# An MoE kernel on one core: the tables of the further token blocks made behind the last expert, and nine unread products at the stage boundary where there were 24

## The chip, the cores and the metric

The kernel runs on one core of a Trainium2 chip. The metric is the device time of one execution in microseconds (us), as the median of three runs; beside it stands one execution that the hardware profiler recorded. Engines are named as the profile names them: PE (TensorE products), PEld (its weight loads), DVE (VectorE), ACT (ScalarE), POOL (GpSimd), SP (SyncE). A name with a q behind it (POOLq, PEldq) is that engine's sequencer, which handles branches, semaphores and drains by itself.

## The reference

One layer: a mixer (gated linear attention beside dilated attention) and, behind it, a mixture of experts with 32 experts, 4 of them for each of 512 tokens, width 1024. Only the second half and the last norm bear on the change. Cut to that:

```python
def moe(xn, router_w, router_b, w_gate_up, b_gate_up, w_down, b_down):
    logits = (xn @ router_w + router_b).astype(jnp.float32)
    top_v, top_e = lax.top_k(logits, TOP_K)              # 4 of 32 experts for each token
    gates = jax.nn.softmax(top_v, axis=-1)
    ...
    def expert_block(args):
        xb, e = args
        h = xb @ w_gate_up[e] + b_gate_up[e]
        gate = jnp.minimum(h[:, ::2], SWIGLU_LIMIT)
        up = jnp.clip(h[:, 1::2], -SWIGLU_LIMIT, SWIGLU_LIMIT)
        act = (up + 1.0) * (gate * jax.nn.sigmoid(SWIGLU_ALPHA * gate))
        return act @ w_down[e] + b_down[e]
    ...                                                  # each token: weighted sum over its 4 experts

h = h + moe(rmsnorm(h, norm_ffn_g), ...)
return rmsnorm(h, norm_final_g)
```

## The kernel before

The program is a row of stages. At the end of each, `stage` (L131) clears the semaphores of the stage and puts a barrier of all engines; the block of instructions that a stage consists of ends with a drain on each engine and a barrier of its own (L1277 for the stage that mixes and routes, L2047 for the experts' stage).

The stage `mix_and_route` ends with the router. DVE takes the top four of each token, counts each token's rank within its expert, and writes the addresses and records of a table of slots (L1668 to L1674). An expert has 96 first slots (`FIRST_SLOTS`). Should an expert have more tokens than that, the rest go through "further" blocks, which are run behind everything else, and only if there are any. Their tables are made by DVE: `further_places` (L1780) counts the blocks of each expert, writes their number to `n_further`, and gives each token beyond the 96 its place; `further_experts` (L2003) writes the expert of each further block. Before the change, the first is the last thing on DVE in `mix_and_route` (L1675), and the second stands on DVE behind the fourth chunk of expert 0 (L2164, L2165).

On PE the same stage ends with `no_work(24)` (L1458): 24 products of 512 columns whose result nobody reads. POOL ends it with the indirect gather of expert 0's rows (L1775).

The stage `experts` streams the weights of 32 experts as 12 chunks of 1 MB each through a ring of eight buffers. ACT rounds a chunk to its high half (`hi`, L1724), DVE subtracts to get the low half (`lo`, L1729), and PE multiplies rows-high by both halves and rows-low by the high half: `gate_up_chunk` (L1881, L1884) eight times for an expert, `down_chunk` (L1894, L1899) four times. In the meantime POOL scatters the table of slots with 16 small indirect transfers (L1759), reads it back, and then gathers each expert's rows (L1775) and adds each expert's output to the totals in memory (L1838). Experts 2 to 29 are in a loop of four to a turn. For the last expert the output isn't scattered: PE turns its one-hot matrix (L2240), DVE copies that out of PSUM (L2177), and PE adds the outputs with it (L2021, L2026). Then come the totals, the last norm (L2200, five instructions on DVE), and the stores.

Behind that, every engine runs `when_any` (L2300): it loads `n_further` from memory into a register (L2302), compares and branches (L2303) to the further blocks or past them. With these inputs no expert has over 96 tokens, so each engine takes the branch past them, and ends the stage with its drain (L2047).

## Time and profile before

| | us |
|---|---|
| median of 3 runs (lowest, highest) | 1821.55 (1821.44, 1821.83) |
| the profiled execution | 1821.84 |
| its span, first to last instruction | 1820.0 |
| PE busy in the span | 1790.7 (98%) |
| DVE, ACT, POOL busy | 1381.0, 1100.2, 141.1 |

The span is 1.8 us shorter than the execution's own time, and that execution is 0.29 us over the median. The mixer and the router take the span up to the boundary at 679 us; the experts' stage takes the rest. In the tables of the profile, busy is what an engine computes; waiting, branches and drains aren't counted, so that an engine can hold up a barrier without being busy.

### The profile page before, as it was taken

The numbers are of one execution on the slowest core, as the hardware profiler recorded it, in microseconds if no ns is written. First come the engines' busy times: TensorE is split into PE (matmuls) and PEld (weight loads), VectorE is DVE, ScalarE is ACT, GpSimd is POOL, SyncE is SP. The second block draws the span as 40 slices with busy tenths as digits, with TensorE's granted clock in tenths as the row PEclk, the third lists the DMA queues.
The fourth block names the chain that finished last, engine by engine and source line by source line (L and its number), as shares of the span: only waits on it lengthen the run. The fifth ranks groups of instructions, "written<-read, shape, count | busy, mean of one in ns | idle before, by whom it ended". The sixth has DMA issues, their size and how long they took to land.

```text
span 1820.0 us, 25032 instructions
## 1 busy us (share of the span) xinstructions
PE 1790.7 (98%) x9119; PEld 1472.9 (81%) x9120; DVE 1381.0 (76%) x1265; ACT 1100.2 (60%) x994; POOL 141.1 (8%) x120
## 2 busy tenths in 40 slices
PE   9999999999999999999999999999999999999996
PEld 7877788898888877788888888888888888888885
DVE  4256344337323568999999999999999999999997
ACT  4253222238331346777777777777777777777774
POOL 1000000000000017110000000000000000000001
PEclk9999999999999999999999999999999999999998
DMA  5321322211323558999999999999999999999993
GB/s 187 124 92 47 127 94 92 84 56 56 120 93 139 180 229 305 378 389 379 383 372 368 387 376 373 381 386 368 380 380 375 373 387 376 373 389 375 375 382 124
DMA packets 100601, 493.95 MB, mean 271 GB/s; under 512 B 15562, under 2 KB 17610, under 8 KB 51008
## 3 DMA queue, kind: packets, MB, share of 16 engines
q1 hardware_dynamic: 90640, 475.97, 68.3%
q0 software_dynamic: 9616, 16.62, 3.6%
q8 instruction: 37, 0.61, 0.1%
q10 hardware_dynamic: 288, 0.59, 0.1%
q14 instruction: 20, 0.16, 0.0%
HBM read 484.40 MB, written 25.21 MB: 280 GB/s over the span
## 4 chain that ended last, share of the span: by engine, by line
PE 58%; POOL 1%; DMA 1%; issue 1%; DVE 1%; ACT 0%; DVEq 0%; POOLq 0%
PE psum L1881 24%; PE psum L1894 12%; PE psum L1884 12%; PE psum L1899 6%; POOL slots_of_experts L1759 1%; PE psum L1853 1%; PE psum L1845 1%; PE psum L1874 1%; DMA h_sb<-normed_rows,row_index 1%; DMA slots_of_experts<-choice_token_and_weight,choice_row_of_table 0%; DMA lists_of_experts<-slots_of_experts 0%; DVE expert_chunk L2032 0%; DVE h_sb L2200 0%; DVE expert_lo L1729 0%; ACT expert_hi L1724 0%
## 5 line engine op out<-in xcount | busy, mean ns | idle before, releaser
L1729 DVE TENSOR_TENSOR expert_lo<-expert_chunk,expert_hi 128x2048 fp32r<-128x2048 f32 x384 | 865.7, 2284 | 45.2 <-ACT expert_hi L1724 42.6
L1724 ACT CAST expert_hi<-expert_chunk 128x2048 fp32r<-128x2048 f32 x384 | 734.9, 1916 | 225.8 <-PE psum L1884 187.6
L275 DVE TENSOR_TENSOR chunk_lo<-chunk,chunk_hi 128x2048 fp32r<-128x2048 f32 x48 | 109.9, 2290 | 252.9 <-ACT chunk_hi L271 252.7
L1881 PE MATMUL psum<-expert_hi,rowsT_hi 128*128 128x512 f32 x992 | 272.0, 396 | 0.0
L1884 PE MATMUL psum<-expert_lo,rowsT_hi 128*128 128x512 f32 x992 | 265.5, 389 | 0.5 <-DVE expert_lo L1729 0.5
L1881 PE MATMUL psum<-expert_hi,rowsT_lo 128*128 128x512 f32 x992 | 265.6, 389 | 0.0
L1884 PEld LDWEIGHTS psum<-expert_lo,rowsT_hi 128*128 128x128 f32 x992 | 186.1, 188 | 40.0 <-DVE expert_lo L1729 1.4
L1881 PEld LDWEIGHTS psum<-expert_hi,rowsT_lo 128*128 128x128 f32 x992 | 186.2, 188 | 39.6
L1881 PEld LDWEIGHTS psum<-expert_hi,rowsT_hi 128*128 128x128 f32 x992 | 181.5, 188 | 41.9 <-issue 7.6
L271 ACT CAST chunk_hi<-chunk 128x2048 fp32r<-128x2048 f32 x48 | 91.8, 1912 | 185.5 <-PE psum L306 158.1
L306 PE MATMUL psum<-chunk_hi,xT_hi 128*128 128x512 f32 x480 | 189.2, 394 | 4.3 <-ACT qk_rows_then_probsT L1070 1.7
L306 PE MATMUL psum<-chunk_hi,xT_lo 128*128 128x512 f32 x480 | 187.5, 391 | 0.0
L306 PE MATMUL psum<-chunk_lo,xT_hi 128*128 128x512 f32 x480 | 187.3, 390 | 0.0
L1894 PE MATMUL psum<-expert_hi,activationsT_hi 128*128 128x512 f32 x496 | 155.9, 396 | 0.0
L1894 PE MATMUL psum<-expert_hi,activationsT_lo 128*128 128x512 f32 x496 | 153.0, 390 | 0.0
L1899 PE MATMUL psum<-expert_lo,activationsT_hi 128*128 128x512 f32 x496 | 132.6, 389 | 0.0
L306 PEld LDWEIGHTS psum<-chunk_hi,xT_hi 128*128 128x128 f32 x480 | 98.0, 204 | 21.7 <-ACT qk_rows_then_probsT L1070 2.1
L306 PEld LDWEIGHTS psum<-chunk_hi,xT_lo 128*128 128x128 f32 x480 | 97.9, 204 | 16.4
L306 PEld LDWEIGHTS psum<-chunk_lo,xT_hi 128*128 128x128 f32 x480 | 98.0, 204 | 15.8
L1894 PEld LDWEIGHTS psum<-expert_hi,activationsT_lo 128*128 128x128 f32 x496 | 93.1, 188 | 20.0
L1899 PEld LDWEIGHTS psum<-expert_lo,activationsT_hi 128*128 128x128 f32 x496 | 93.1, 188 | 19.3
L1894 PEld LDWEIGHTS psum<-expert_hi,activationsT_hi 128*128 128x128 f32 x496 | 90.8, 188 | 17.2
(299 smaller groups left out, 1888.2 us busy)
## 6 DMA issues: line engine op xcount, KB each, us to landing
expert_chunk<-in_expert_w_gate_up SPq DMA_DIRECT2D x256, 1024.0 KB, 7.8
expert_chunk<-in_expert_w_down SPq DMA_DIRECT2D x128, 1024.0 KB, 6.9
chunk<-in_w_in SPq DMA_DIRECT2D x38, 1024.0 KB, 5.0
chunk<-in_w_branch_gla SPq DMA_DIRECT2D x4, 1024.0 KB, 5.0
chunk<-in_w_mix_out SPq DMA_DIRECT2D x4, 1024.0 KB, 5.1
gla_v<-in_x SPq DMA_DIRECT2D x4, 512.0 KB
y_glaT_away<-h_sb SPq DMA_DIRECT2D x1, 2048.0 KB, 7.7
att_qT_then_y_glaT<-y_glaT_away SPq DMA_DIRECT2D x1, 2048.0 KB, 7.6
```

Of the source, the lines that this page charges most:

```text
L271: act.copy(self.whi[c][:], self.raw[c][:]).then_inc(self.hi_done[c], 1)
L275: dve.tensor_tensor(self.wlo[c][:], self.raw[c][:], self.whi[c][:].bitcast(F32), ALU.subtract).then_inc(self.lo_done[c], 1)
L306: last = pe.matmul(bank, stationary, moving, start=(k == 0 and n == 0), stop=(k == KT - 1 and n == 2))
L1724: act.copy(self.expert_hi[c % self.SLOTS][:], self.expert_ring[c % self.RING][:]).then_inc(self.moe["hi"], 1)
L1729: dve.tensor_tensor(self.expert_lo[s][:], self.expert_ring[c % self.RING][:], self.expert_hi[s][:].bitcast(F32), ALU.subtract).then_inc(se ...
L1759: pool.indirect_dma_start(self.table, bass.IndirectOffsetOnAxis(ap=self.address[:, b, j:j + 1], axis=0), self.record[:, b, j, :], None, bo ...
L1845: last = pe.transpose(turned(f)[:, k, :], rows[taken, (HALF_KT * f + k) * P:(HALF_KT * f + k + 1) * P], self.ident[taken, taken])
L1853: last = pe.transpose(turned(f)[:, k, :], a[taken, (HALF_KT * f + k) * P:(HALF_KT * f + k + 1) * P], self.ident[taken, taken])
L1881: pe.matmul(bank, x[:, k, :], whi[s][:, m // 2, m % 2 * COLS:(m % 2 + 1) * COLS], start=False, stop=False)
L1884: last = pe.matmul(bank, rows_hi[:, k, :], wlo[s][:, m // 2, m % 2 * COLS:(m % 2 + 1) * COLS], start=False, stop=(k == KT - 1))
L1894: pe.matmul(bank, x[:, 2 * q + kk, :], whi[s][:, kk, m * COLS:(m + 1) * COLS], start=(q == 0 and kk == 0 and x is acts[0]), stop=False)
L1899: last = pe.matmul(bank, acts[0][:, 2 * q + kk, :], wlo[s][:, kk, m * COLS:(m + 1) * COLS], start=False, stop=(q == 3 and kk == 1))
```

## The change

- `further_places` goes from the end of `mix_and_route` to the end of the experts' stage on DVE, behind the four chunks of the last expert's down projection and ahead of the copy of the turned one-hot matrix. The wait for `tables_in` goes there too.
- `further_experts` goes from behind the fourth chunk of expert 0 to behind the last norm on DVE. Behind it DVE increments a new semaphore, `tables_made`.
- `when_any` now waits for `tables_made` on all five engines, ahead of the load of `n_further`.
- `no_work(24)` at the end of `mix_and_route` on PE becomes `no_work(9)`.

```diff
                 self.list_rows(pe, 0)
-                no_work(24)
+                no_work(9)
...
                 dve.tensor_tensor(self.record[:, :, :, 1], ex[:], tot[:].unsqueeze(2).to_broadcast([P, NB, TOP_K]),
                                   ALU.mult).then_inc(E_S["records"], 1)
-                self.further_places(dve)
...
                 lo(dve, 3)
-                dve.wait_ge(S["tables_in"], 32)
-                further_experts(dve)
                 for c in range(SLOTS, GU):
                     lo(dve, c)
...
                 for c in range(first, first + 4):
                     lo(dve, c)
+                self.further_places(dve)
+                dve.wait_ge(S["tables_in"], 32)
                 dve.wait_ge(S["hot_turned"], 1)
                 dve.tensor_copy(hotT[:], self.bank[6].rearrange("p (b n) -> p b n", n=P)).then_inc(S["hotT"], 1)
...
                         dve.scalar_tensor_tensor(out=fin[b][:, at], in0=self.total_sb[b][:, at], scalar=rs[:, b:b + 1],
                                                  in1=self.h[:, 3, at], op0=ALU.mult, op1=ALU.mult).then_inc(S["done"], 1)
+                further_experts(dve)
+                dve.sem_inc(S["tables_made"], 1)
                 further_dve(dve)
...
         def when_any(engine, body, first=None, then=None):
 
+            engine.wait_ge(self.moe["tables_made"], 1)
             n = engine.value_load(self.n_further[0:1, 0:1], min_val=0, max_val=self.FURTHER)
```

The next rows are the order of instructions on DVE in the built programs. The line numbers are those of each program (after the change they are one or two off), and the names behind "waits" are partly those under which an earlier stage used the same semaphore. First the end of routing and the start of the experts' stage, before the change:

```order
L1672 COPY choice_token_and_weight<-token_numbers_sb 128x16
L1673 TENSOR_TENSOR choice_token_and_weight<-top_exps,top_sums 128x16
L1784 TENSOR_SCALAR extra_blocks<-tokens_of_expert 128x32
L1786 TENSOR_SCALAR past<-tokens_of_expert 128x32 [waits chain_dve]
...
L1797 TENSOR_TENSOR place_in_further<-place_in_further,beyond_first_block 128x128 [waits chain_dve]
L1798 TENSOR_SCALAR place_in_further<-place_in_further 128x128 [waits chain_dve]
L1277 UNCONDITIONAL_BRANCH [waits chain_dve]
L2154 UNCONDITIONAL_BRANCH [waits barrier_Pool_Activation_PE_DVE_SP_release]
L1729 TENSOR_TENSOR expert_lo<-expert_chunk,expert_hi 128x2048 [waits gla_small_in]
```

and after it:

```order
L1672 COPY choice_token_and_weight<-token_numbers_sb 128x16
L1673 TENSOR_TENSOR choice_token_and_weight<-top_exps,top_sums 128x16
L1277 UNCONDITIONAL_BRANCH
L2153 UNCONDITIONAL_BRANCH [waits barrier_Pool_Activation_PE_DVE_SP_release]
L1728 TENSOR_TENSOR expert_lo<-expert_chunk,expert_hi 128x2048 [waits gla_small_in]
```

The 17 instructions of `further_places`, each of which waits for the one ahead of it, are gone from between the records and the branch that ends the stage. Now DVE behind the last expert's four chunks, before the change:

```order
L1729 TENSOR_TENSOR expert_lo<-expert_chunk,expert_hi 128x2048 [waits gla_small_in] x4
L2177 CAST slots_one_hotT<-psum 128x512 [waits gla_cleared]
```

and after it:

```order
L1728 TENSOR_TENSOR expert_lo<-expert_chunk,expert_hi 128x2048 [waits gla_small_in] x4
L1783 TENSOR_SCALAR extra_blocks<-tokens_of_expert 128x32
L1785 TENSOR_SCALAR past<-tokens_of_expert 128x32 [waits chain_dve]
...
L1796 TENSOR_TENSOR place_in_further<-place_in_further,beyond_first_block 128x128 [waits chain_dve]
L1797 TENSOR_SCALAR place_in_further<-place_in_further 128x128 [waits chain_dve]
L2176 CAST slots_one_hotT<-psum 128x512 [waits gla_cleared,x_turned,chain_dve]
```

The same 17 stand here now, ahead of the copy, which has two more semaphores to wait for. Last, the end of DVE's program, behind the last norm, as the change makes it; before it, the load of `further_blocks` stood right behind the L2200 rows and waited for nothing:

```order
L2199 SCALAR_TENSOR_TENSOR gate_values<-expert_chunk,total_rstd,h_sb 128x512
L2004 TENSOR_TENSOR blocks_before<-past,block_starts_sb 128x672
L2006 TENSOR_REDUCE block_expert_f<-blocks_before 128x21 [waits chain_dve]
L2007 TENSOR_SCALAR further_block_expert<-block_expert_f 128x21 [waits chain_dve]
L2304 TENSOR_LOAD further_blocks [waits chain_dve,moe_tables_made]
L2304 ISA x2
L2305 COMPARE_AND_BRANCH
```

On POOL the same load stands behind the four powers of the last norm:

```order
L2118 TENSOR_TENSOR total_rstd<-total_sum_squares,minus_half 128x1 [waits gla_y_out] x3
L2304 TENSOR_LOAD further_blocks [waits gate_up_lo,moe_tables_made]
L2304 ISA x2
L2305 COMPARE_AND_BRANCH
```

What moved is the wait: PE, ACT, POOL and SP go through the same load, two register instructions and branch as before, but each of them now behind DVE's `tables_made`.

## Rows read from the trace of the kernel before

**Rows 1.** The page, part 4: share of the chain that ended last, by engine

```profile
PE 58%; POOL 1%; DMA 1%; issue 1%; DVE 1%; ACT 0%; DVEq 0%; POOLq 0%
```

**Rows 2.** Waits of PE from 679 to 1800 us: total, times, longest

```profile
PE psum L1874 <- DVE rowsT_lo L1866: 1.0, 1, 1.0
```

**Rows 3.** Line 1277, sequencers: xcount: ns min/median/max, first to last start

```profile
L1277 POOLq DRAIN  x1: 4651/4651/4651, 672.1 to 672.1; - x1
L1277 PEldq DRAIN  x1: 5165/5165/5165, 673.4 to 673.4; - x1
L1277 DVEq DRAIN  x1: 10/10/10, 677.9 to 677.9; - x1
```

**Rows 4.** Timeline at the boundary, PE and POOL: start, us, engine, line [idle before]

```profile
670.71 7.87 PE L229 MATMUL psum<-ones_r 128*128 128x512 f32 x24
682.84 1.15 PE L1881 MATMUL psum<-expert_hi,activationsT_hi 128*128 128x512 f32 x4 [1.06 <-issue]
672.32 1.24 POOL L1775 DMA_INDIRECT h_sb<-normed_rows,row_index  x1 [5.43 <-issue]
```

**Rows 5.** Timeline at the boundary, DVE

```profile
673.60 0.16 DVE L1673 TENSOR_TENSOR choice_token_and_weight<-top_exps,top_sums 128x16 f32<-128x16 f32 x1
677.38 0.23 DVE L1798 TENSOR_SCALAR place_in_further<-place_in_further 128x128 f32<-128x128 f32 x1
679.51 2.29 DVE L1729 TENSOR_TENSOR expert_lo<-expert_chunk,expert_hi 128x2048 fp32r<-128x2048 f32 x1 [1.90 <-PEq L137]
681.72 1.01 DVE L1866 TENSOR_TENSOR activationsT_lo<-psum,activationsT_hi 128x384 fp32r<-128x384 f32 x2
```

**Rows 6.** Stretches: PE, PEld, DVE, ACT, POOL busy (instructions), clock, DMA, GB/s

```profile
668.50:675.30 6.80, 6.80 (x19) 5.17 (x18) 5.15 (x21) 5.27 (x6) 1.24 (x1) 0.50 0.07 16
675.40:678.60 3.20, 3.18 (x14) 2.26 (x13) 1.93 (x9) 0.00 (x0) 0.00 (x0) 1.00 0.09 37
```

**Rows 7.** Timeline of DVE in expert 0

```profile
691.43 0.85 DVE L2005 TENSOR_TENSOR blocks_before<-past,block_starts_sb 128x672 f32<-128x672 f32 x1
693.42 6.70 DVE L1729 TENSOR_TENSOR expert_lo<-expert_chunk,expert_hi 128x2048 fp32r<-128x2048 f32 x3
703.45 2.29 DVE L1729 TENSOR_TENSOR expert_lo<-expert_chunk,expert_hi 128x2048 fp32r<-128x2048 f32 x1 [1.17 <-ACT expert_hi L1724]
```

**Rows 8.** Timeline of POOL and DVE while the table of slots is written

```profile
703.85 2.75 POOL L1759 DMA_INDIRECT slots_of_experts<-choice_token_and_weight,choice_row_of_table  x1 [0.31 <-issue]
706.90 0.98 POOL L1759 DMA_INDIRECT slots_of_experts<-choice_token_and_weight,choice_row_of_table  x1 [0.30 <-issue]
```

**Rows 9.** Timeline of DVE behind the last expert

```profile
1787.63 8.89 DVE L1729 TENSOR_TENSOR expert_lo<-expert_chunk,expert_hi 128x2048 fp32r<-128x2048 f32 x4
1800.61 0.69 DVE L2177 CAST slots_one_hotT<-psum 128x512 fp32r<-128x512 f32 x1 [4.10 <-PE psum L2240]
1813.08 1.41 DVE L2200 SCALAR_TENSOR_TENSOR gate_values<-expert_chunk,total_rstd,h_sb 128x512 f32<-128x512 f32 x2
```

**Rows 10.** Lines 2302 and 2303, sequencers: the load of further_blocks, the branch

```profile
L2302 PEldq TENSOR_LOAD <-further_blocks x1: 486/486/486, 1802.9 to 1802.9; - x1
L2302 POOLq TENSOR_LOAD <-further_blocks x1: 499/499/499, 1811.7 to 1811.7; - x1
L2303 PEldq COMPARE_BRANCH  x1: 3654/3654/3654, 1803.8 to 1803.8; - x1
```

**Rows 11.** Line 2047, sequencers: the drains that end the experts' stage

```profile
L2047 PEldq DRAIN  x1: 73/73/73, 1807.5 to 1807.5; - x1
L2047 POOLq DRAIN  x1: 6513/6513/6513, 1812.6 to 1812.6; - x1
L2047 SPq DRAIN  x1: 7/7/7, 1817.3 to 1817.3; - x1
```

**Rows 12.** DMA issues from 679 to 1820 us: xcount, median us to landing

```profile
h_sb<-normed_rows,row_index POOLq DMA_INDIRECT x31
residual_rows<-h_sb,row_index POOLq DMA_INDIRECT x31, 10.0
```

More of the change, by code:

```diff
@@ L214, in build @@
                         "x_turned", "x_hi", "x_lo", "cleared", "passed", "weights_out", "hot_turned", "hotT", "y_hi",
-                        "y_lo", "totals", "padded", "table_cleared", "records", "placed", "lists_in", "half_set", "summed", "squared", "means", "powed", "done")}
+                        "y_lo", "totals", "padded", "table_cleared", "records", "placed", "lists_in", "half_set", "summed", "squared", "means", "powed", "done", "tables_made")}
                     self.residual_stored, self.normed_stored = self.sem("residual_stored"), self.sem("normed_stored")
```

## The prediction

> **What bounds the kernel now.** I read the page's chain first: PE takes 58% of it and no other engine over 1% [rows 1], so a microsecond counts where PE stands, or where nobody works because all wait for a barrier. The change touches two such places and a stretch between them. For the stretch I asked for PE's waits: in 1120 us of experts the longest but one is 1.0 us, at expert 2 [rows 2]. The rest is products one behind another, so the experts' stage is a block that slides with its start. The two places are its ends, and there the busy rows don't help, since drains aren't busy time; the sequencers' rows do.
>
> At the first boundary the barrier opens when the last engine has drained. A drain's row gives its start and its length, and the sum is when the engine was really done: PE 673.4 + 5.2 = 678.6, DVE 677.9, POOL 672.1 + 4.65 = 676.7 [rows 3]. PE is last, because of its 24 unread products, which run from 670.7 to 678.6 [rows 4]. DVE's last table instruction ends at 677.6, and its first work behind the barrier starts at 679.5 [rows 5]. So PE binds by 0.7 us over DVE and by 1.9 over POOL. POOL's row is the one to note: its last work is the gather of expert 0's rows, issued at 672.3 and generated by 673.6 [rows 4], and its drain still takes until 676.7.
>
> At the end of the kernel the same reading gives PE 1807.5 + 0.07 and SP 1817.3, but POOL 1812.6 + 6.5 = 1819.1 [rows 11], 0.9 us ahead of the span's end of 1820.0. So POOL's drain, which no table of busy time shows, ends the kernel. It starts that early because POOL loads the block count at 1811.7 [rows 10], right behind its last power, waiting for nobody.
>
> **The change, part by part.**
>
> The first boundary. `further_places` goes: DVE's records end at 673.8 instead of the tables at 677.6, 3.8 us earlier [rows 5]. PE's nine products: they start at 670.7 as before, and the clock is at 0.50 until 675.3 [rows 6]. At full clock a product takes 3.20 / 14 = 0.23 us; the other 10 of the 24 took the 4.6 us from 670.7 to 675.3, 0.46 each [rows 4, 6]. Nine take 4.1, so PE is done at about 674.9. POOL isn't touched: its gather waits for an index that DVE makes ahead of all this, so its drain ends at 676.7 as before. Now that one is last, and the barrier opens 678.6 - 676.7 = 1.9 us earlier, not the 3.7 us that PE and DVE leave room for. Bounds: 0 if POOL's drain has something in it that waits for the others, 3.7 if it goes with them. I take 1.9, since both of its rows are untouched. Behind the barrier the first low half and the turned rows' low half stand on DVE (679.5 to 682.7) [rows 5], and PE waits 1.06 us for them until 682.84 [rows 4]; this order stays, so all 1.9 us arrive at PE: **-1.9**.
>
> The clock. Before, PE ran products without a pause from 670.7, and the clock rose at 675.3 [rows 4, 6]; in the changed kernel the products end 0.4 us short of that, and then PE stands still until the barrier has opened, at about 677.6. If the clock isn't up by 680.9, when the first expert's products start, they run at half speed until it is. Lower bound 0, the clock rises as before. Upper bound: it needs the same 4.6 us of unbroken work again, counted from 680.9, and half of 4.6 is lost, 2.3 us; counted from the stage's start at 677.6 it is up at 682.2 and costs 0.65. There is little slack in which to make it good, the 1.0 us at expert 2 [rows 2], and even that hangs on a chain of POOL's which begins with PE's list for expert 1, behind the second chunk. In the likeliest case I put it at **+0.2**, near its lower end.
>
> `further_experts` leaves expert 0. It took 691.43 to 693.42, 2.0 us [rows 7]. Nothing comes of it: twelve microseconds later DVE stands for 1.17 us waiting for ACT, whose turn follows PE's [rows 7], so what DVE gains it waits away. There is a side effect to weigh. POOL writes the table of slots just then, and one such transfer takes 2.75 us where a low half runs on DVE (703.45 to 705.74) and 0.98 where none does [rows 7, 8]. The three table instructions left POOL alone; now the low halves come 2 us earlier and the gap behind them is 2 us longer. Sum of gaps the same, and both orders meet at the transfer under the low half of 703.45. **0**, bounds -0.5 to +0.5 (the wait of 1.0 us at expert 2 is all that could be won [rows 2]).
>
> `further_places` at its new place. DVE's four low halves end at 1787.63 + 8.89 = 1796.5, and the copy of the one-hot matrix waits 4.10 us for PE, until 1800.6 [rows 9]. The 17 instructions took 3.8 us behind one another [rows 5] and end at about 1800.4. They fit, with 0.2 us to spare for one more wait: **0**, at most +0.2. With that cover gone they'd cost up to 3.8.
>
> The end. Last on DVE is the norm's final piece, which ends at 1813.08 + 1.41 = 1814.5 [rows 9]. Behind it now `further_experts`, 2.0 us [rows 7], and the increment: `tables_made` is there at about 1816.5. What is queued behind the new wait on each engine is the load, the branch and the drain. POOL takes 0.95 us from load to drain (1811.7 to 1812.6) [rows 10, 11]: its drain starts at 1817.45. If it takes 6.5 us as before it ends at 1823.95, **+4.85**. PE is next: from the load at 1802.9 to the drain's end at 1807.6 are 4.65 us, 3.65 of them in the branch [rows 10, 11], hidden before behind the last norm. Now they end at 1821.15: without POOL the end would come +2.0 later. SP adds some 1.3 us of load and branch and is done before 1818. So POOL decides, and the question is whether those 6.5 us are work of the drain or a wait for something else. POOL issued 31 gathers, 31 scatters [rows 12] and 17 transfers for the table in this stage, 79 in all, and 6513 / 79 is 82 ns each; at the first boundary only one was out. A pass over what was issued would start when the drain starts, and would be as long as now. Bounds: 0 for the drain (the others' are 7 and 73 ns [rows 11]), and then PE's +2.0 is the end; 6.5 the other way. I take 6.5, its own row.
>
> Two rules of the Trainium skill bear on this. PE's branch took 3654 ns [rows 10], where POOL goes from its load through its branch to its drain in 0.95 us; "Runtime: NRT & Kernel Launch", section "Instruction fetch mechanics", says that a taken branch to a target outside the fetched window stalls until the page has been brought in. By that rule, the trace agrees, PE pays this again wherever its wait stands. POOL's drain took 6513 ns [rows 11]; "VectorE: DVE Perf Modes", section "The DRAIN you can't avoid", says that the drains of the frame around a program take about 12 ns each on all five engines. By that rule the drain's length is no work, the end would be PE's, and the kernel would come out level; the row of 6513 is against it as far as it goes.
>
> The sum is -1.9 + 0.2 + 0 + 0 + 4.85 = +3.15, so 1825.0 for the profiled execution of 1821.84. The median of the runs was 0.29 lower, and I predict for it: 1821.55 + 3.15 = 1824.7. A difference under 0.2%, 3.6 us, can't be told from none here.
>
> **Rivals.**
>
> First, the drain waits for something that the change doesn't move, and PE's branch is the end. This is the case that comes out not slower: -1.9 + 2.0 + 0 to 0.2, about 1821.8. For it: 6.5 us is long for an engine that has only four powers behind it, and 1819.1 is two microseconds behind the landing of the last store, which SP sees at 1817.3. Against it: the other long drain of POOL also went on for 3 us behind its last instruction, with no store near it [rows 3, 4], and nothing else of POOL's is out at the end. It decides if the drain's row in the changed kernel is shorter than 3.7 us. If PE's branch stall shrank too, it would be 1820.
>
> Second, the forecast with the clock low at the first expert, by the place and the price above: half rate from 680.9 for 1.3 to 4.6 us, +0.65 to +2.3 on top of +2.95, 1825.2 to 1826.8, about 1826.0. For it: nine products end before the clock rose in the trace of before, and the few ahead of them, from 668.5 on, had not raised it [rows 6]. Against it: 0.4 us is little, and one more turn of the unread products follows the barrier.
>
> Third, the change doesn't do what it says at the front: POOL's drain ends later for a reason that I don't see, and the barrier opens as before. Then only the end is left, 1821.55 + 4.85 = 1826.4.
>
> **How the numbers follow.** Forecast 0.42, 1824.7, its own range 1824.2 to 1825.3. First rival 0.25, 1820 to 1822.5. Second 0.27, 1825.2 to 1826.8. Third 0.06, 1826.4. The range takes in the forecast, the second and third, and the better part of the first: 1821.4 to 1826.8. Slower by over 0.2% is above 1825.2: most of the second rival, the third, and a little of the forecast, 0.34. Faster by over 0.2%, under 1817.9, none of the cases reaches: 0.03 for what I have overlooked. Within 0.2%: 0.63.
>
> **What would show it.** The first barrier: POOL's drain ends last, near 676.7, and DVE's first low half starts near 677.6 instead of 679.5. The end: five loads of `further_blocks` within 0.1 us of each other, about 2 us behind the last norm; PE's branch of about 3.6 us; POOL's drain of about 6.5 us, ending last. The forecast is wrong if that drain is short, or if the first products of expert 0 stand at twice 0.23 us each.

## The result, and the profile after

The changed kernel takes 1827.51 us (median of nine runs, 1826.39 to 1829.17), against 1821.58 for the kernel before on the same chip (nine runs, 1821.44 to 1822.01). The ratio is 1.0031, with a 95% interval of 1.0022 to 1.0040: it is slower by 5.9 us (4.0 to 7.3 by the interval). The forecast was 1824.7 and its range ended at 1826.8. The direction of the likeliest case was right, and the size was too small by 2.8 us. Two things stand beside each other here: the end, which came as forecast, and the middle, which did not.

The profiled execution of the changed kernel took 1828.05 us, with a span of 1826.3. Its line numbers are one or two lower than those of before (L1728 for L1729) or higher (L2304 for L2302).

**The front.** The sequencers' rows of the barrier's line in the changed kernel (count, ns, start), which answer to [rows 3]:

```profile
L1277 PEldq DRAIN  x1: 5180/5180/5180, 669.9 to 669.9; - x1
L1277 POOLq DRAIN  x1: 4581/4581/4581, 672.4 to 672.4; - x1
L1277 DVEq DRAIN  x1: 1267/1267/1267, 672.9 to 672.9; - x1
```

PE is done at 675.1, DVE at 674.1, and POOL at 672.4 + 4.6 = 677.0: POOL's drain is the last, as the prediction had it, and 0.3 us later than it had it. The DMA issues from 672.6 to 677.1 us tell what this drain waits for (the last number is the us from issue to landing):

```profile
h_sb<-normed_rows,row_index POOLq DMA_INDIRECT x1, 4.3
```

The gather of expert 0's rows is issued at 672.68 and has landed at 676.93, and the drain is over 81 ns later. In each of the twelve traces that hold this landing the drain ends 80 or 81 ns behind it. The timeline of PE behind it, with DVE's first low half (start, us, engine, line, then the idle time before it):

```profile
677.93 0.65 PE L1873 MATMUL psum<-bias_rows,ones_r 32*128 32x512 f32 x4 [2.85 <-PEq L137]
681.59 1.08 PE L1880 MATMUL psum<-expert_hi,activationsT_hi 128*128 128x512 f32 x4
```

```profile
677.93 2.29 DVE L1728 TENSOR_TENSOR expert_lo<-expert_chunk,expert_hi 128x2048 fp32r<-128x2048 f32 x1 [3.84 <-PEq L137]
```

The stage starts at 677.93 and not 679.51 [rows 5], 1.58 us earlier. But PE stood still for 2.85 us before it, where it was 0.93 us before. The windows tell what the clock did (the number ahead of the last two is the granted clock; these answer to [rows 6]):

```profile
668.00:674.70 6.70, 6.70 (x21) 5.47 (x20) 4.28 (x15) 5.74 (x6) 1.24 (x1) 0.50 0.08 21
674.80:678.10 3.30, 0.45 (x6) 0.20 (x4) 0.17 (x1) 0.00 (x0) 0.09 (x1) 1.00 0.19 65
678.20:681.50 3.30, 3.30 (x16) 2.66 (x13) 3.30 (x4) 0.96 (x2) 2.60 (x6) 0.50 0.48 181
746.50:749.70 3.20, 3.20 (x11) 2.24 (x8) 3.20 (x3) 1.12 (x2) 0.00 (x0) 0.50 0.98 394
```

The clock rose to its full 2.4 GHz at 674.7, nearly as the forecast had it. Then it stood at full while PE did nothing, and behind the pause it fell to 1.2 GHz for 3.4 us. That cost little here, since the fall ended at 681.6, where the first expert's products begin, and the slow products ahead of them filled time in which PE had waited for 1.06 us before the change: 681.59 for 682.84 [rows 4], so 1.25 of the 1.58 us arrive. The fourth row is another fall that the kernel before doesn't have, 65 us later, at expert 2.

**Expert 2.** PE's waits from 640 to 1800 us (total, times, longest), which answer to [rows 2]:

```profile
PE psum L1873 <- PEq L137: 2.9, 1, 2.9
PE psum L1873 <- DVE rowsT_lo L1865: 1.8, 1, 1.8
```

The one wait of 1.0 us that the prediction had called slack has become 1.8 us. DVE's row where it takes the lists of rows, first in the kernel before, then in the changed one:

```profile
729.25 0.15 DVE L1767 CAST row_index<-lists_of_experts 128x1 int32<-128x1 f32 x1 [2.18 <-DMA lists_of_experts<-slots_of_experts]
```

```profile
728.65 0.15 DVE L1766 CAST row_index<-lists_of_experts 128x1 int32<-128x1 f32 x1 [2.90 <-DMA lists_of_experts<-slots_of_experts]
```

DVE stands at this row until POOL's read of the lists has landed, with all its low halves queued behind. They came only 0.60 us earlier, and DVE waited 2.90 us for them instead of 2.18. PE in the changed kernel:

```profile
746.26 0.70 PE L1873 MATMUL psum<-bias_rows,ones_r 32*128 32x512 f32 x4 [1.80 <-DVE rowsT_lo L1865]
746.88 2.08 PE L1880 MATMUL psum<-expert_hi,rowsT_hi 128*128 128x512 f32 x4
750.18 1.07 PE L1883 MATMUL psum<-expert_lo,rowsT_hi 128*128 128x512 f32 x4
```

Before, the first of these stood at 746.84, so 0.58 us is left of the front's gain. The second row shows four products in 2.08 us where four at full clock take 1.07: the clock fell 0.15 us behind the pause of 1.80 us and came back 3.4 us later. By expert 3's first products the changed kernel is 0.94 us behind the kernel before (782.55 for 781.61), where it was 0.58 ahead at expert 2's: the fall cost 1.5.

**The end.** DVE's last norm and what is now behind it, then the loads and the drains (these answer to [rows 9], [rows 10] and [rows 11]):

```profile
1802.03 0.69 DVE L2176 CAST slots_one_hotT<-psum 128x512 fp32r<-128x512 f32 x1 [0.72 <-PE psum L2241]
1814.50 1.41 DVE L2199 SCALAR_TENSOR_TENSOR gate_values<-expert_chunk,total_rstd,h_sb 128x512 f32<-128x512 f32 x2
1815.83 0.85 DVE L2004 TENSOR_TENSOR blocks_before<-past,block_starts_sb 128x672 f32<-128x672 f32 x1
1817.60 0.18 DVE L2007 TENSOR_SCALAR further_block_expert<-block_expert_f 128x21 int32<-128x21 f32 x1
```

```profile
L2304 POOLq TENSOR_LOAD <-further_blocks x1: 497/497/497, 1817.9 to 1817.9; - x1
L2305 PEldq COMPARE_BRANCH  x1: 344/344/344, 1818.8 to 1818.8; - x1
```

```profile
L2046 POOLq DRAIN  x1: 6513/6513/6513, 1818.8 to 1818.8; - x1
L2046 PEldq DRAIN  x1: 72/72/72, 1819.2 to 1819.2; - x1
L2046 SPq DRAIN  x1: 13/13/13, 1819.4 to 1819.4; - x1
```

The norm ends at 1815.91, 1.43 us later than before. POOL's drain starts at 1818.84, 2.93 us behind the norm's end; before, it started 1.85 us ahead of it. That is 4.78, against the 4.85 of the prediction. The drain's length is the same to the nanosecond.

The ledger of the two profiled executions: expert 2's first products -0.58, the fall of the clock there +1.5, and +0.5 in the last expert (from its first products to the one-hot copy are 46.64 us for 46.19), together +1.43 at the norm's end; the end +4.78; sum +6.2, as the two executions differ (1828.05 for 1821.84).

### The profile page after: what moved, and what is told of

Its sections match the earlier page's. It is cut to its first block, busy times and chain, and to the rows that moved or that the text cites. A ratio compares the mean times of both kernels' runs of the same rounds, so it can differ in the third digit from the quotient of the medians.

```text
span 1826.3 us, 25002 instructions
## 1 busy us (share of the span) xinstructions
PE 1789.9 (98%) x9104; PEld 1472.2 (81%) x9105; DVE 1381.6 (76%) x1265; ACT 1100.8 (60%) x994; POOL 139.8 (8%) x120
## 4 chain that ended last, share of the span: by engine, by line
PE 58%; DVE 1%; POOL 1%; issue 1%; DMA 1%; ACT 0%; POOLq 0%; DVEq 0%
PE psum L1880 24%; PE psum L1893 12%; PE psum L1883 12%; PE psum L1898 6%; POOL slots_of_experts L1758 1%; PE psum L1852 1%; PE psum L1844 1%; PE psum L1873 1%; DVE expert_lo L1728 1%; DMA slots_of_experts<-choice_token_and_weight,choice_row_of_table 0%; DMA lists_of_experts<-slots_of_experts 0%; DVE expert_chunk L2031 0%; DVE h_sb L2199 0%; PE psum L2020 0%; POOL total_rstd L2118 0%
## 5 line engine op out<-in xcount | busy, mean ns | idle before, releaser
L1728 DVE TENSOR_TENSOR expert_lo<-expert_chunk,expert_hi 128x2048 fp32r<-128x2048 f32 x384 | 866.2, 2286 | 49.1 <-ACT expert_hi L1723 44.7
```

The source lines that it names most:

```text
L1728: dve.tensor_tensor(self.expert_lo[s][:], self.expert_ring[c % self.RING][:], self.expert_hi[s][:].bitcast(F32), ALU.subtract).then_inc(se ...
```

## The experiments

Fifteen runs followed, on four chips; e12 is the changed kernel again, and e15 repeats e9. On these chips the kernel before spread more than on the first one, from 1820.8 to 1825.2 us, with medians of 1822.3 to 1822.9, so each time is given beside the kernel before of its own chip, and the traces decide where a difference is under 2 us. Names: "later take" is the edit of e5. The intervals are for the ratio, 95%.

**e1, 24 products in the changed kernel.**

```diff
-                no_work(9)
+                no_work(24)
```

> The changed kernel with 24 unread products ahead of the barrier, not nine; the tables stay behind the last expert. Theory A, the clock: what the changed kernel lost beyond the end (about 2.9 us) comes of the pause that PE makes between its nine products and the first work behind the barrier. With 24 PE is the last to drain again (about 678.6), the clock rises once near 675 and stays, PE's wait at expert 2 is back to about 1.0 us: the front's gain goes and the loss in the middle goes too, 1821.6 + 4.8 = 1826.4, and the times lie within 0.6 us as before the change. Theory B, the order: the loss in the middle comes of further_experts having left expert 0 (the low halves there run earlier against POOL's transfers, so the lists come late). Then the wait at expert 2 stays near 1.8 us or more and the time is 1821.6 + 4.8 + about 1.5 to 3 = 1828 to 1829.4.

Measured: 1828.15 against 1822.88, ratio 1.0026 (1.0015 to 1.0037). The times don't separate the theories: 5.3 us above its own before, where theory A has 4.8 and the changed kernel 5.9, and the interval is 4 us wide. The trace does, and theory A is wrong as an account of the middle: PE pauses 0.93 us at the barrier and the clock stays up there, yet it waits 1.9 us at expert 2, and the clock falls at 748.3 for 3.4 us:

```profile
746.79 0.50 PE L1873 MATMUL psum<-bias_rows,ones_r 32*128 32x512 f32 x4 [1.89 <-DVE rowsT_lo L1865]
```

The absolute time lies in theory B's range only because the kernel before is 1.3 us slower on this chip; 5.3 is less than B's 6.4 to 7.8. B's reason is tested by POOL's rows: from the first of the 16 table transfers to the last are 34.84 us in this trace, and 34.84 in the kernel before. So `further_experts` in expert 0 neither helps nor hurts POOL.

**e2, nine products in the kernel before.**

```diff
-                no_work(24)
+                no_work(9)
```

> The kernel before with nine unread products, not 24; all tables stay where they were. DVE is then the last to drain, 677.9, 0.7 us ahead of PE's 678.6. Theory A (clock): PE stands still from about 675 to the barrier, the clock falls again behind it, and 0.7 us won are lost two or three times over: 1822 to 1824, with a wider spread. Theory B (order): nothing in the middle changes, -0.7, 1820.9.

Measured: 1823.24 against 1822.88 (median of ten; an eleventh execution took 9124.92 us and is left out), ratio 1.0003 (0.9994 to 1.0013). No difference by the times. The trace shows what the 0.6 us at the front turned into: PE paused 3.84 us, and the clock, which hadn't risen yet, stayed at half until 683.7.

```profile
678.92 0.80 PE L1874 MATMUL psum<-bias_rows,ones_r 32*128 32x512 f32 x4 [3.84 <-PEq L137]
682.75 1.53 PE L1881 MATMUL psum<-expert_hi,activationsT_hi 128*128 128x512 f32 x4
```

POOL's 16 transfers took 35.77 us, 0.9 longer, and the lists came at 730.4. Both the wait (1.87 us) and the fall at expert 2 are there, with the tables where they always were.

**e3, the tables where DVE was thought to have room.** `further_places` in expert 30 behind the fifth low half, `further_experts` and the increment ahead of the one-hot copy.

> The changed kernel with further_places in the middle of expert 30 and further_experts, with the increment of tables_made, in DVE's wait for the one-hot matrix: the tables are there at about 1800, so POOL's load waits for nobody. If the 4.8 us at the end are the delayed start of POOL's drain and nothing else, they go whole: 1827.5 - 4.8 = 1822.7, with POOL's drain of 6.5 us starting near its 1812.6. If the 17 + 3 instructions aren't hidden there, up to 3.8 us come back and the one-hot copy on DVE starts later than 1.4 us against the kernel before.

Measured: 1824.61 against 1822.88, ratio 1.0008 (0.9999 to 1.0017): 1.7 us above its own before, where the changed kernel stands 5.9. POOL's drain starts 1.84 us ahead of the norm's end again, so the end's 4.8 us go whole. The places aren't free, though. Of PE's waits the second is for an activation that DVE made late, behind the 17 table instructions; the first is for the rows of expert 2, whose gather took 11.7 us from issue to landing where it takes 8.3 in the changed kernel's trace, long before the tables' new places:

```profile
PE psum L1844 <- DMA h_sb<-normed_rows,row_index: 3.2, 1, 3.2
PE psum L1852 <- DVE h_sb L1976: 0.9, 1, 0.9
```

From expert 31's first products to the one-hot copy are 47.43 us here, 46.64 in the changed kernel and 46.19 in the kernel before.

**e4, the kernel before with a wait at the end alone.**

```diff
+                dve.sem_inc(S["tables_made"], 1)      # behind the last norm
                 further_dve(dve)
...
+            engine.wait_ge(self.moe["tables_made"], 1)
```

> The kernel before with the tables where they were, and the increment of tables_made behind the last norm, for which all five engines wait ahead of the load: it prices the wait at the end by itself. If POOL's drain is 6.5 us from wherever it starts: increment at 1814.5, drain from 1815.45 to 1821.95, 1821.6 + 2.85 = 1824.4. If it waited for something unmoved: 1821.6 to 1822. PE's branch takes 0.35 us (as in the changed kernel) and not 3.65, as the wait gives its fetch time.

Measured: 1823.65 against 1822.88, ratio 1.0005 (0.9996 to 1.0014): less than expected. The trace says why, and it is the expectation's mistake. DVE's increment doesn't wait for the norm's last write: the loads stand at 1813.3, while that write ends at 1815.37. POOL's drain starts 0.65 us ahead of the norm's end, 1.2 us later than before in that measure, and is 6513 ns long. PE's branch took 4.53 us here, so the wait ahead of it isn't enough to bring the 344 ns of the changed kernel; what they go with is said below.

**e5, the later take.** In expert 0, DVE takes expert 2's row numbers behind the low half of chunk 7 instead of ahead of it.

```diff
-                if q == 6 and more:
+                if q == (6 if e0 else 7) and more:
                     list_take(dve, e + 2, (e0 + 2) % self.UNROLL, reused=e0 > 1)
```

> The kernel before with one edit: in expert 0 DVE takes expert 2's row numbers one low half later (behind that of chunk 7, not ahead of it), so that the late lists don't hold up the low halves. Theory C, the lists: in every trace so far expert 2's first products start 17.6 us after DVE takes the lists, since DVE works without a pause in between; PE's wait there is the lateness of the lists. Then DVE gains its 2.2 us of idle time, PE's wait of 1.0 to 1.9 us goes, and the time falls by 1.0 or more, the slower executions the most. Theory A (the clock at the front alone): no change. If the gather of expert 2's rows is late in its turn, PE waits for it instead, 0.2 to 1 us at the transposes.

Measured: 1820.44 against 1822.45, ratio 0.9994 (0.9986 to 1.0003; one run of 1828.5 is in it). Nine of twelve runs lie between 1820.11 and 1820.88, but the interval takes in 1, so the trace has to show it. It has no wait of PE's at expert 2 at all, and DVE's 2.2 us have become 0.54:

```profile
729.78 0.15 DVE L1767 CAST row_index<-lists_of_experts 128x1 int32<-128x1 f32 x1 [0.54 <-DMA lists_of_experts<-slots_of_experts]
```

Theory C is shown: what PE waits for at expert 2 is the lists, through DVE's order.

**e6, the later take in the changed kernel.**

> The changed kernel with the same one edit. Theory C: PE's wait of 1.8 us at expert 2 goes and with it the 3.4 us at half clock behind it, worth 1.7: -3.5, 1827.5 to about 1824.0. Then what is left over the kernel before is the end's 4.8 less the front's 1.6 to 1.9, less the 1.0 that was won at expert 2. Theory A (the front's pause costs it): the loss stays, 1827 to 1828.

Measured: 1825.62 against 1822.45, ratio 1.0022 (1.0012 to 1.0031), 3.2 us above its own before where the changed kernel stands 5.9, so 2.7 went and not the 3.5 expected. The wait at expert 2 and the fall there are gone. The rest is at the front, where in this execution the fall lasted twice as long:

```profile
677.50:684.10 6.60, 6.22 (x22) 4.90 (x23) 6.16 (x6) 0.96 (x2) 5.34 (x7) 0.50 0.67 204
```

Against e5's trace this one starts the stage 1.55 us earlier and expert 31 0.02 us later (1752.99 for 1752.97), so the fallen clock cost 1.6 us. That is the second rival's mechanism, and a price inside its 0.65 to 2.3. The norm ends 0.49 us later than in e5, which is the price of `further_places`.

**e7, a longer pause on purpose.** Two more subtractions of 128x384 on DVE ahead of expert 2's low halves, in the kernel before.

> The kernel before with two more subtractions of 128x384 on DVE, into a tile that nobody reads, ahead of expert 2's low halves: 0.9 to 1.0 us more of PE's pause there, 1.9 instead of 1.0. If the pause makes the clock fall: +0.95 for the pause and +1.7 for 3.4 us at half rate, +2.6, 1824.2 on the chip of the first runs. If it doesn't: +0.95, 1822.6.

Measured: 1823.99 against 1822.45, ratio 1.0006 (0.9998 to 1.0015). Inconclusive: in the profiled execution the gather of expert 2's rows was late as well, so the pause came in two pieces of 1.39 and 1.22 us with 6.4 us of products between them, and the clock stayed up.

**e8, no powers on POOL.** The powers are replaced by copies on ACT, so this kernel leaves out the power that makes the last norm's scale.

> The kernel before without the four powers of the last norm; ACT copies the mean squares instead (so the output is not the reference's). POOL then has nothing behind the scatter of expert 30, and loads, branches and drains some 8 us earlier. If its drain is 6.5 us of work from wherever it starts, it ends by about 1811, SP's drain at 1817.3 is the last, and the kernel ends 1.8 us earlier. If the drain waits for the stores or for something else at the end, it gets longer, ends near 1819.1 as before, and nothing is won.

Measured: 1819.89 against 1822.45, ratio 0.9986 (0.9977 to 0.9995). The drains in its trace:

```profile
L2047 POOLq DRAIN  x1: 6513/6513/6513, 1799.5 to 1799.5; - x1
L2047 SPq DRAIN  x1: 13/13/13, 1817.2 to 1817.2; - x1
```

POOL drains 13 us earlier for the same 6513 ns, and SP's store is the end. The drain doesn't wait for the stores, which come behind its end. This trace also holds a pause of 1.81 us at expert 2 behind which the clock did not fall.

**e9 and e15, roots on ACT.** The kernel before with the later take, and with the last norm's four powers taken from POOL.

```diff
-                    pool.tensor_tensor(rs[:, b:b + 1], ss[:, b:b + 1], half[:], ALU.pow).then_inc(S["powed"], 1)
+                            act.activation(rs[:, m:m + 1], ss[:, m:m + 1], ACT.Sqrt).then_inc(S["powed"], 1)
...
+                    dve.reciprocal(rs[:, b:b + 1], rs[:, b:b + 1]).then_inc(S["inverted"], 1)
```

> The kernel before with expert 2's row numbers taken one low half later and, for the last norm, square roots on ACT and reciprocals on DVE in place of the four powers on POOL; all outputs are computed. POOL then loads, branches and drains behind the scatter of expert 30, near 1799. If the 6.5 us are work from wherever the drain starts, SP's drain is the last: 1.8 us less than with the later take alone (1820.4), about 1818.7. If the chain of root, reciprocal and two semaphores is longer than the power's, a few tenths come back. If the drain at the end waits for something else, nothing is won.

> The kernel before with the later take and the roots on ACT, again on this chip: 1818.8 (1817.8 to 1820.9 the first time), 1.8 us under the same without the roots, 3.5 under the kernel before.

Measured: 1818.79 against 1822.32, ratio 0.9982 (0.9973 to 0.9991), and on another chip 1818.55 against 1822.63, ratio 0.9984 (0.9975 to 0.9993). This version beats both kernels: it is 3.5 to 4.1 us faster than the one before. In e9's trace POOL's drain is over at 1804.2, and the norm ends at 1813.16, 0.14 us later than in e5, while the span is 1.9 us shorter.

**e10, e11, e13 and e14: can the early barrier pay?** All have the change's tables behind the last expert, and the later take. e11 and e14 keep the end's wait; e10 and e13 have `further_experts` and the increment ahead of the first total instead; e13 has the roots on ACT too.

> The changed kernel with 18 unread products, the later take, and further_experts with the increment in DVE's 1.4 us wait ahead of the first total, not behind the last norm. The early barrier is kept (DVE's first low half near 677.9), the clock doesn't fall at either place, and tables_made is there by 1806. Expected: the later take's 1820.4, less 1.6 at the front, plus 0.3 for further_places and 0.5 for further_experts over its wait: 1819.6. If products up to the barrier don't keep the clock up, 2.5 us more.

> The changed kernel with 18 unread products and the later take: against the changed kernel with the later take and nine (median 1825.6, clock at half from 677.4 to 684.2 in its trace) it shows what the clock costs at the first expert alone. If the pause of 3.2 us between nine products and the first work behind the barrier makes it fall, 18 keep it up and 2.0 to 2.5 us go: 1823.3. If the clock there falls whatever the number, 1825.6 stays.

> The changed kernel with 22 unread products, the later take, further_experts in DVE's wait ahead of the first total, and the roots on ACT, so that no drain of POOL's stands at the end. If the early barrier pays when PE has work nearly up to it: PE's products end near 677.5, the pause is about 1.5 us, the clock stays up, 1 us is won at the front and 0.8 paid for the tables: level with the kernel that keeps its tables ahead of the barrier and has the other two edits (1818.8), 1818.6. If 22 are still too few, the clock falls and it is 1819.5 to 1820.5.

> The changed kernel with 24 unread products and the later take. PE's drain is the last again, the pause 0.9 us, the clock stays up; barrier as in the kernel before. If the nine products' early barrier is worth nothing (it wins 1.6 us and the fallen clock takes it back), the time is that of the same kernel with nine or 18, 1825.5. If the early barrier pays, it is up to 1.6 us slower, 1827; if the clock costs more than the barrier gives, 1824.5.

| kernel | unread products | median | kernel before, same chip | ratio (95%) | pause at the barrier | clock behind it |
|---|---|---|---|---|---|---|
| e6 | 9 | 1825.62 | 1822.45 | 1.0022 (1.0012 to 1.0031) | 3.17 | falls, 6.8 us |
| e11 | 18 | 1825.41 | 1822.32 | 1.0022 (1.0011 to 1.0033) | 2.28 | falls, 3.4 us |
| e14 | 24 | 1826.15 | 1822.63 | 1.0020 (1.0011 to 1.0029) | 0.93 | stays |
| e10 | 18 | 1820.94 | 1822.32 | 0.9995 (0.9987 to 1.0004) | 2.70 | falls, 3.4 us |
| e13 | 22 | 1819.28 | 1822.63 | 0.9990 (0.9979 to 1.0001) | 0.93 | stays |

e6, e11 and e14 stand 3.2, 3.1 and 3.5 us above their own before: whether the barrier opens early or late, no difference can be told, and the medians lie within 0.4 us. It is also what the parts give: 4.8 for the end and 0.5 for `further_places`, less the 2.0 of e5, are 3.3. 18 products weren't enough, since in e10's execution the clock was at full already when they ran, and they were done at 674.4:

```profile
670.03 4.35 PE L229 MATMUL psum<-ones_r 128*128 128x512 f32 x18
680.40 1.89 PE L1880 MATMUL psum<-expert_hi,activationsT_hi 128*128 128x512 f32 x4 [0.51 <-issue]
```

e10 and e13 fell short of what was expected of them by 1.3 and 0.7 us. e13 against e15 on one chip is the change without its price at the end: 1819.28 against 1818.55, nothing won by moving the tables. In their traces the stage starts 0.47 us earlier in e13 and expert 31 0.33 us, so here, where no clock fell, most of the front's gain gets through; but from there to the norm's end the tables cost 1.1 us, where 0.8 had been allowed for them.

e11's profiled execution took 1834 us, and shows a rare cost of the later take. POOL's gather for expert 2:

```profile
729.69 7.62 POOL L1774 DMA_INDIRECT h_sb<-normed_rows,row_index  x1 [6.07 <-DVE row_weight L1767]
```

It took 7.62 us, where it takes 1.06 or 1.07 in the other seven traces with the later take and 2.29 with the early one. DVE's three low halves in a row ran from 729.70 to 736.4 beside it, and PE waited 6.2 us for the rows. The same three low halves start within 0.01 us of the gather in the other seven traces too. What differs is who is held up: there the first of them takes 2.32 or 2.33 us and the gather 1.07, here the low half takes 2.28 and the gather lasts until all three are done. Ten of the 90 runs with the later take lie 6 to 9 us over the median of their kernel; of the 131 runs of the kernel before none lies over 1825.2. Which of the two goes first isn't settled by any run.

**e12, the changed kernel again.**

> The changed kernel again, on the chip of the other three, for comparison: 1827.5 as before, 5.9 us over the kernel before or a little less where that one is slower. Its trace shows which of the two falls of the clock repeat: at the first expert, behind a pause of 2.9 us, yes; at expert 2 it depends on how late the lists land, and the wait is 1.4 to 2.0 us.

Measured: 1827.55 against 1822.32, ratio 1.0029 (1.0019 to 1.0040). The same time, put together otherwise: the clock was at half for 6.8 us at the first expert, there was no fall at expert 2, and POOL's chain was hit. Its gather for expert 1 waits for an index that hangs on a product of PE's:

```profile
677.90:684.50 6.60, 6.58 (x23) 5.15 (x24) 6.52 (x6) 0.96 (x2) 5.55 (x7) 0.50 0.67 239
```

```profile
690.38 2.28 POOL L1774 DMA_INDIRECT h_sb<-normed_rows,row_index  x1 [1.93 <-DVE row_weight L1752]
```

## Why the prediction was wrong, by its own steps

**The front, -1.9.** Right in its mechanism: POOL's drain became the last, and the barrier opened 1.58 us earlier. The lower bound had asked whether this drain waits for something. It does, for the landing of the gather (81 ns before its end), and the gather wasn't moved by the change.

**"This order stays, so all 1.9 us arrive at PE", and the experts' stage as "a block that slides with its start".** This is the step that failed. It doesn't slide, because expert 2 hangs on another chain: 16 table transfers on POOL, the read of the lists, and DVE's take, behind which DVE works without a gap. From the take to expert 2's first products are 17.59 to 17.61 us in all seven traces with the early take and nothing else in the way (before, changed, e1, e2, e4, e8, e12). In the kernel before this chain is the later one by 0.98 us. The prediction read that 0.98 as slack to be won back; it is the margin by which the other chain binds, and PE can arrive as early as it likes. The front's gain gets through only as far as the lists come earlier. POOL's chain began 1.58 us earlier, but took 0.26 longer. Then the way from the last transfer to the take was 13.89 us against 13.17; in the nine traces with the early take it lies between 13.05 and 13.94, at both ends of that with the tables in either place, so nothing ties that part to the change. 0.60 was left.

**The clock, +0.2.** Right that it would rise by the time of the first products, and wrong in what it looked at. It weighed only whether the clock comes up late. What happens is that PE, with nine products, stands still before the barrier, and the clock falls again. In the 17 traces a pause of 0.93 to 1.48 us at the barrier was followed by no fall (ten); of the seven of 2.28 to 3.84, six were followed by one, and in the seventh, e2, the clock had never risen. The price in PE's own products, as the way from the stage's start to expert 1's first products (29.97 to 30.04 us in the ten traces without a fall), is 0.3 to 0.9 us in the changed kernel, e2, e10 and e11 and 1.7 to 1.8 in e3, e6 and e12, where the clock was low for 6.8 us. POOL's chain pays too: its 16 transfers take 34.84 to 34.91 us in the ten traces without a fall, wherever the tables stand, and 35.10 to 36.65 in the seven with a low clock. The prediction had named that link (the list for expert 1 behind the second chunk) and not priced it. The +0.2 was put near the lower end of its bounds; in e3, e6 and e12 it came to 1.7 to 1.8, of the 2.3 that was the upper one.

**A second fall, at expert 2.** It wasn't in the sum. Pauses of 0.98 to 1.39 us there left the clock up. Behind the ones of 1.80, 1.87, 1.89, 3.20 and 6.16 it fell, and behind one of 1.81 it didn't. The price is 1.5 to 1.6 us between the first products of expert 2 and expert 3 (changed kernel, e1, e2). Why 1.80 was followed by a fall and 1.81 not isn't shown; e7, which was to test it, gave two shorter pauses. These terms may also be what spreads the changed kernel's times over 2.8 us; no run shows that.

**`further_experts` out of expert 0, 0.** Right (e1 and the kernel before: 34.84 us both).

**`further_places` in the wait of 4.10 us, 0 to +0.2.** It took 3.9 us and ended at 1801.3; the copy came 0.72 us behind it and PE waited 0.3 us for it. In all it cost 0.5 us (46.64 for 46.19 us from expert 31's first products to the copy), so its upper bound of 0.2 was too low.

**The end, +4.85.** Right, at 4.78. The question between forecast and first rival was whether the drain's 6.5 us are work. They are 6513 ns in all 17 traces, from starts between 1797.6 and 1825.1, and e8 and e9 show that it doesn't wait for the stores. The first rival is refuted. One of the prediction's grounds against it was no ground, though: the long drain of POOL at the first barrier is a wait, for the gather's landing. The rule of the Trainium skill that was set against this row ("VectorE: DVE Perf Modes", section "The DRAIN you can't avoid") gives about 12 ns for the drains of a program's preamble and postamble. The drains of L2047 end a block of the kernel itself, so that rule wasn't one for them; SP's 7 to 13 ns and ACT's 8 are of its size, and POOL's 6513 are not. What sets the length isn't shown: no run changed the number of transfers that POOL had issued. PE's branch was expected at 3.65 us again, by the rule of the Trainium skill in "Runtime: NRT & Kernel Launch", section "Instruction fetch mechanics", that a taken branch stalls when its target isn't in the part of the program that has been fetched. It took 344 ns in the changed kernel. Over the 17 traces it is 340 to 344 ns in the five of kernels with nine unread products (changed, e2, e3, e6, e12) and 3.4 to 5.0 us in the twelve with 18, 22 or 24. With fewer instructions of PE's ahead of it the target lies elsewhere in the program, which would fit the rule; no run moved the target alone, so that isn't shown. The mistake was to carry the row of one program over to another. It decided nothing in any run, as PE's drain was never the last at the end.

**The sum by the steps.** Forecast: -1.9 + 0.2 + 0 + 4.85 = +3.15. The two profiled executions: -0.58 at expert 2's first products (1.3 more than the front's term), +1.5 by the clock at expert 2 (1.3 more than the clock's term), +0.5 in the last expert, +4.78 at the end; in all +6.2, and 5.9 in the medians. In e12 the second fall is missing, but expert 2's first products start 0.11 us later than in the kernel before: the low clock at the first expert has eaten the front's whole gain through POOL's chain. That the two losses take turns like this is read from two traces of the changed kernel; in which share of the runs each comes isn't known.

## What to carry to other kernels

A short wait on the binding engine in an otherwise gapless stretch marks the place where another chain binds. Before counting a gain upstream as delivered, follow that wait back through every engine to what it hangs on; if that chain doesn't start earlier as well, the gain becomes a longer wait. And where filler work ahead of a barrier is taken away, look at how long the engine will stand still, not at when it is done: here the clock, where it was up, fell behind every pause of 2.28 us or more, and that took back 0.3 to 1.8 us. Drains belong in the ledger: the engine whose drain is long should have its last work early. Moving four small powers off POOL was worth 1.5 to 2.1 us here (e9 and e15 against e5, each over its own before), as much as the 1.9 that the whole change aimed at.

## What the runs showed that I had not expected

- POOL's drain at the end of the kernel is 6513 ns in every trace, from any start. At the first barrier it is 4.5 to 5.0 us, and ends 80 or 81 ns behind the landing of the one gather that is out.
- TensorE's clock was at full and fell to half at pauses of 2.3 to 3.2 us (six of six at the barrier) and 3.2 and 6.2 us at expert 2, and behind three of 1.80 to 1.89 us and not behind one of 1.81. In some it fell before the pause was over, in others up to 1.5 us behind it. It came back 3.4 to 10.2 us later.
- An increment on DVE placed behind the last norm was seen by the other engines 2 us before the norm's last write had ended (e4: loads at 1813.3, write until 1815.4).
- PE's branch past the further blocks took 340 to 344 ns in the five traces of kernels with nine unread products and 3.4 to 5.0 us in the twelve with more.
- The same gather on POOL took 1.07, 2.29 or 7.62 us. With the same three low halves on DVE beside it, it took 1.06 or 1.07 in seven traces and 7.62 in one.
